# One level of Strassen's scheme for the gate and up products of a streaming encoder layer

## The reference, cut to what matters

```python
h = _rmsnorm(y, norm1_g)
fq, fk, fv, logf, gq, gk, gv, glog, gr = _project(h, w_in, ...)
fox_o = _fox_prompt(...)            # forgetting attention (and _fox_sample)
gla_o, S = _gla_prompt(...)         # gated linear attention
y = y + _merge(fox_o, gla_o, gr, gla_norm_g, w_out)     # silu(gr) gates gla_o
y = y + _swiglu(_rmsnorm(y, norm2_g), w_gate, w_up, w_down)
y = _rmsnorm(y, final_norm_g)

def _swiglu(h, w_gate, w_up, w_down):
    return (jax.nn.silu(h @ w_gate) * (h @ w_up)) @ w_down
```

## Time and profile before

| | us |
|---|---|
| median of 3 runs | 3361.66 (3357.69 to 3363.92) |
| profiled execution | 3358.64 |
| its span (first to last instruction) | 3356.9 |
| busy PE | 3084.2 (92% of the span) |
| busy PE weight loads | 2852.9 (85%) |
| busy DVE | 2053.2 (61%) |
| busy ACT | 1188.7 (35%) |
| busy POOL | 508.0 (15%) |

### The profile page before, as it was taken

How to read it: one execution, slowest core, us unless ns; L and a number is a source line. 1 busy time by engine, 2 the same in 40 slices (tenths; PEclk the granted TensorE clock), 3 DMA queues, 4 the chain that set the end, 5 groups by cost and what they waited for, 6 DMA issues and landing times. The chain is left out here.

```text
span 3356.9 us, 49447 instructions
## 1 busy us (share of the span) xinstructions
PE 3084.2 (92%) x18905; PEld 2852.9 (85%) x18905; DVE 2053.2 (61%) x3540; ACT 1188.7 (35%) x2361; POOL 508.0 (15%) x404
## 2 busy tenths in 40 slices
PE   7999999959999956889978999999998999999996
PEld 5899999947777734677768999999998999999995
DVE  5232212759999833677744666666666666666665
ACT  6353111238888712444432222222224322222223
POOL 0010000000000001321202222222222322222223
PEclk9999999969999977899998999999999999999998
DMA  4235422253242082344435111111133311111112
GB/s 123 73 135 185 148 58 58 51 114 83 63 96 63 1 266 66 111 140 141 144 100 176 51 44 44 50 44 46 48 127 115 107 50 44 44 50 44 44 37 77
DMA packets 280252, 290.37 MB, mean 86 GB/s; under 512 B 32473, under 2 KB 246806, under 8 KB 271040
## 3 DMA queue, kind: packets, MB, share of 16 engines
q1 hardware_dynamic: 277464, 281.12, 28.8%
q10 hardware_dynamic: 1344, 4.36, 0.6%
q0 software_dynamic: 1296, 2.88, 0.3%
HBM read 200.40 MB, written 87.92 MB: 86 GB/s over the span
## 5 line engine op out<-in xcount | busy, mean ns | idle before, releaser
L2376 PE MATMUL ps_ffn<-h,wsp_n 128*128 128x312 f32 (+1 forms) x6336 | 1048.7, 321 | 23.9 <-DMA h<-h2T 23.0
L2376 PEld LDWEIGHTS ps_ffn<-h,wsp_n 128*128 128x128 f32 x6336 | 1011.4, 189 | 27.4 <-issue 23.4
L2302 DVE TENSOR_TENSOR yacc<-ps_ffn,yacc 128x312 f32<-128x312 f32 (+1 forms) x1008 | 489.5, 519 | 386.2 <-PE ps_ffn L2394 386.1
L660 PE MATMUL ps_project<-hT,wsp 128*128 128x416 f32 (+1 forms) x3000 | 602.1, 357 | 0.0
L660 PEld LDWEIGHTS ps_project<-hT,wsp 128*128 128x128 f32 (+1 forms) x3000 | 548.2, 186 | 23.5 <-issue 7.8
L2394 PE MATMUL ps_ffn<-aT,dsp 128*128 128x312 f32 (+1 forms) x3168 | 550.1, 323 | 4.0 <-DVE yacc L2302 3.1
L2394 PEld LDWEIGHTS ps_ffn<-aT,dsp 128*128 128x128 f32 x3168 | 509.5, 189 | 8.0 <-DVE yacc L2302 3.7
L2278 ACT ACTIVATE aT<-a 128x416 fp32r<-128x416 f32 x132 | 65.1, 494 | 821.1 <-DVE a L2353 821.1
L2181 POOL TENSOR_TENSOR wsp_n<-wraw_n,wsp_n 128x1024 fp32r<-128x1024 f32 x88 | 211.8, 2408 | 815.7 <-ACT wsp_n L2222 815.7
L2344 DVE RECIPROCAL silu<-silu 128x416 f32<-128x416 f32 x132 | 304.9, 2310 | 30.1 <-ACT silu L2267 30.0
L1001 ACT ACTIVATE pexp<-ps_fox,ntop 128x512 f32<-128x512 f32 (+2 forms) x320 | 198.6, 621 | 52.9 <-DVE ntop L1044 51.1
(11 more groups left out here) (258 smaller groups left out, 3447.3 us busy)
## 6 DMA issues: line engine op xcount, KB each, us to landing
wraw_n<-in_w_gate_dram SPq DMA_DIRECT2D x44, 512.0 KB, 3.9
wraw_n<-in_w_up_dram SPq DMA_DIRECT2D x44, 512.0 KB, 3.8
draw<-in_w_down_dram SPq DMA_DIRECT2D x44, 512.0 KB, 3.4
h2T<-hT_m SPq DMA_DIRECT2D x16, 1024.0 KB, 5.3
zT<-zs SPq DMA_DIRECT2D x12, 1040.0 KB, 4.1
wraw<-in_w_in_dram SPq DMA_DIRECT2D x24, 512.0 KB, 4.5
h<-h2T SPq DMA_DIRECT2D x8, 1248.0 KB, 12.6
qk_hi<-work SPq DMA_DIRECT2D x8, 1024.0 KB
```

Source lines behind the costliest of these rows:

```text
L660: last = pe.matmul(ps[0:w, p % NB, 0:BLK], wsp[:, b, s, k, 0:w], hT[:, g * TPB:(g + 1) * TPB, v, k, :], start=k == 0 and m == 0, stop=k == ...
L2302: dve.tensor_tensor(y, z, y, ALU.add).then_inc(added, 1)
L2376: last = pe.matmul(ps[:, 2 * q + s, 0:FB[b] * TT], wsp[:, par, s, w, k, :], h2[:, v, k, cols(b)], start=m == 0, stop=m == 3 * KD - 1)
```

## The change

`ffn` is rewritten. The 2080 tokens are taken in four groups of FT = 520 tokens instead of two halves of 1040, and the 22 tiles of D_FF in 11 pairs: 44 pairs of a group and a pair of tiles. For a pair, the gate product is a product of blocks, (2 tiles of 128) x (2 halves of D_MODEL) times (2 halves of D_MODEL) x (2 halves of 260 tokens), and is made by Strassen's scheme in Winograd's form: 7 products of blocks in place of 8. This is an even cell; the up product of the same pair is the odd cell after it (NCELL = 88). Each of the 7 products (P1 to P7, with operands O_B11 ... O_B22) is 4 blocks of 128 rows by 3 passes = 12 matmuls of 260 columns, into one of 6 PSUM banks. The operands are split to high and low parts as before; four of the weight operands are sums of weight blocks, and four of the h operands are sums of h blocks.

The cells' 8 down items (6 matmuls of 260 columns, into 2 PSUM banks) belong to the pair before and stand between the products. At the end of each group (a turn: the last odd cell of groups 0 to 2) the h operands of the next group are made: they exist once, so each is overwritten when the last product that reads it is done. The rows of a finished group are turned, squared, scaled and stored beside the next group's first cells. The weights pass four times, once per group. All is unrolled; `Fori` is gone.

Sigmoid is one ACT instruction in place of Exp, Identity + 1 and DVE's reciprocal, in `ffn` and in `project`'s gate blocks. h2T holds f32 values once, not a high and a low half; `gla_merge` copies h out on ACT (`rows_h`) and has no `low_h`.

The core of the diff, first what other stages lose or get:

```diff
-                    act.activation(silu, ps[:, p % NB, 0:BLK], ACT.Exp, scale=-1.0).then_inc(s_exp, 1)
-                    act.wait_ge(s_exp, m + 1)
-                    act.activation(silu, silu, ACT.Identity, bias=ones[:]).then_inc(s_one, 1)
+                    act.activation(silu, ps[:, p % NB, 0:BLK], ACT.Sigmoid).then_inc(s_sigmoid, 1)
...
-                dve.wait_ge(s_one, m + 1)
-                dve.reciprocal(silu, silu).then_inc(s_inv, 1)
-                dve.wait_ge(s_inv, m + 1)
+                dve.wait_ge(s_sigmoid, m + 1)
...
-            def low_h(c, e):
-                L = width(c)
-                dve.wait_ge(h_high, 2 * c + e + 1)
-                dve.tensor_tensor(hT[:, LO, 4 * e:4 * e + 4, 0:L], ps[:, B_O, :].rearrange("p (k t) -> p k t", k=4)[:, :, 0:L],
-                                  hT[:, HI, 4 * e:4 * e + 4, 0:L].bitcast(F32), ALU.subtract).then_inc(h_low, 1)
```

The new `ffn` on POOL and ACT:

```diff
+            def low_w(c, i):
+                raw = wsum[:, S_OF[i]] if i in S_OF else wraw[:, c % 2, A_OF[i]]
+                pool.wait_ge(w_hi, NPROD * c + i + 1)
+                pool.tensor_tensor(wop[:, i, LO], raw, wop[:, i, HI].bitcast(F32), ALU.subtract).then_inc(w_lo, 1)
...
+            for c in range(NCELL + 1):
...
+                for i in range(NPROD):
+                    if c + 1 < NCELL:
+                        low_w(c + 1, i)
+                    if i == 1 and c:
+                        low_d(c - 1)
+                    if turn and i in (O_B21, O_T3, O_B22):
+                        low_h(q, i)
...
+            def high_w(c, i):
...
+                if c:
+                    act.wait_ge(product, NPROD * (c - 1) + i + 1)
+                act.activation(wop[:, i, HI], raw, ACT.Copy).then_inc(w_hi, 1)
...
+            for c in range(NCELL):
...
+                first_out(c)
+                for i in range(NPROD):
+                    if c + 1 < NCELL:
+                        high_w(c + 1, i)
+                    if turn:
+                        high_h(q, i)
+                    if i == P5 and c:
+                        high_d(c - 1)
+                    if i >= P2:
+                        if s == 0:
+                            gate_sigmoid(u, i - P2)
+                        else:
+                            high_a(u, i - P2)
```

On DVE, the functions and the order of an odd cell:

```diff
+            def sum_w(c, j):
...
+                if c:
+                    dve.wait_ge(w_lo, NPROD * (c - 1) + {0: P5, 1: P6, 2: P7, 3: P3}[j] + 1)
+                if j == 0:
...
+                    dve.tensor_tensor(wsum[:, 0], wraw[:, b, A21], wraw[:, b, A22], ALU.add).then_inc(w_sum, 1)
...
+            def combine(c, what):
...
+                after = {U2: P6, V2: P6, C11: P2, U3: P7, C22: P7, C21: P4, C12: P3}[what]
+                dve.wait_ge(product, NPROD * c + after + 1)
...
+                dve.tensor_tensor(out, product_bank(c, i), partial, ALU.add).then_inc(combined, 1)
...
+            def make_a(u, j):
...
+                dve.tensor_tensor(x, x, sg[:, j], ALU.mult).then_inc(a_made, 1)
...
+            def low_a(u, j):
+                f, t = PLACE[j]
+                dve.wait_ge(a_hi, 4 * u + j + 1)
+                dve.tensor_tensor(aT[:, u % 2, LO, f, t * FH:(t + 1) * FH], cs[:, 1, f, t * FH:(t + 1) * FH],
+                                  aT[:, u % 2, HI, f, t * FH:(t + 1) * FH].bitcast(F32), ALU.subtract).then_inc(a_lo, 1)
...
+                    if turn:
+                        low_h(q, O_B11)
+                        sum_h(q, O_T1)
+                    item(c, 0)
+                    silu(u, J21)
+                    item(c, 1)
+                    if more:
+                        sum_w(c + 1, 0)
+                        sum_w(c + 1, 1)
...
+                    combine(c, U2)
+                    combine(c, V2)
+                    silu(u, J12)
+                    combine(c, C11)
+                    item(c, 2)
+                    item(c, 3)
+                    make_a(u, J11)
+                    combine(c, U3)
+                    combine(c, C22)
+                    make_a(u, J22)
+                    item(c, 4)
+                    low_a(u, J11)
...
+                    item(c, 5)
+                    if more:
+                        sum_w(c + 1, 2)
+                    combine(c, C21)
+                    make_a(u, J21)
+                    low_a(u, J22)
+                    item(c, 6)
+                    if more:
+                        sum_w(c + 1, 3)
+                    combine(c, C12)
+                    make_a(u, J12)
+                    low_a(u, J21)
+                    item(c, 7)
```

`low_a(u, J12)` stands first in the next even cell. `silu` and `gain` are DVE operations on SBUF operands as well. On PE:

```diff
+            def down(n, u, dd, t):
+                h, c = divmod(dd, 4)
+                pe.wait_ge(a_lo, 4 * u + (J12 if t else J21) + 1)
+                pe.wait_ge(d_lo, 2 * u + h + 1)
+                if n >= 2:
+                    pe.wait_ge(item_out, n - 1)
...
+            for c in range(NCELL):
+                cell_product(c, P1)
+                item(c, 0)
+                cell_product(c, P5)
+                item(c, 1)
+                cell_product(c, P6)
+                cell_product(c, P2)
+                item(c, 2)
+                item(c, 3)
+                cell_product(c, P7)
+                item(c, 4)
+                item(c, 5)
+                cell_product(c, P4)
+                item(c, 6)
+                cell_product(c, P3)
+                item(c, 7)
```

More of the change, by code:

```diff
@@ new lines @@
+FT = NTOK // NG4
+FH = FT // 2
+KH = KD // 2
+NPAIR = DFF // (2 * P)
+NPROD = 7
+O_B11, O_T1, O_T2, O_B21, O_T3, O_T4, O_B22 = range(NPROD)
+P1, P5, P6, P2, P7, P4, P3 = range(NPROD)
+A11, A21, A22, A12 = range(4)
+S_OF = {P5: 0, P6: 1, P7: 2, P3: 3}
+A_OF = {P1: A11, P2: A12, P4: A22}
+NBANK = 6
+J11, J22, J21, J12 = range(4)
+PLACE = {J11: (0, 0), J22: (1, 1), J21: (1, 0), J12: (0, 1)}
+NU = NG4 * NPAIR
+NCELL = 2 * NU
+ITEMS = 8
+NROW = FT // TT
+ROW_AFTER = (0, 1, 3, 5, 6)
+LATE = ((0, 1), (2, 3), (4,))
@@ L2158, in last @@
[L2158 to L2168 removed]
+            ws = [d[n][0].rearrange("(k p) f -> p k f", p=P) for n in ("w_gate", "w_up")]
@@ L2170, in _ @@
+            for t in range(NROW):
+                store(NG4 - 1, t)
+            for t in range(NROW):
+                sp.wait_ge(y_stored[t], 16 * (NG4 + (t == NROW - 1)))
         @block.gpsimd
@@ L2284, in _ @@
+            high_d(NCELL - 1)
+            for k, ts in enumerate(LATE):
+                for t in ts:
+                    for half in range(2):
+                        square(NG4 - 1, t, half, late_row(t, half))
+                root(ts, NG4 - 1 + k)
         @block.vector
         def _(dve):
[L2286 to L2302 removed]
@@ new lines, in _ @@
+            low_a(NU - 1, J12)
+            for k in range(ITEMS):
+                add(late_down(0, k), False, k, 0)
+            for k in range(ITEMS):
+                add(late_down(1, k), False, k, 1)
+                if k % 2:
+                    t, half = divmod(k // 2, 2)
+                    row(late_row(t, half), NG4 - 1, t, half)
+            n = NG4 - 1
+            sum_squares(LATE[0], n, 2 * NROW * n + 4)
+            row(late_row(2, 0), n, 2, 0)
+            row(late_row(2, 1), n, 2, 1)
@@ L2413, in step @@
-            def step(u, par, off, gu, down):
-                half = u // NF if isinstance(u, int) and u in (0, NF) else None
-                for slot in range(SLOTS):
-                    if gu:
-                        gate_up(u, par, slot // 2, slot % 2, half)
-                    rows(u, GU, slot)
-                    if down:
-                        downs(u, 1 - par, slot)
-                    rows(u, DN, slot)
-            steps(pe, lambda: None, step, lambda: None)
+            pe.wait_ge(filled, 3)
@@ new lines, in cell_product @@
+            def cell_product(c, i):
+                u, s = divmod(c, 2)
+                q = u // NPAIR
+                pe.wait_ge(w_lo, NPROD * c + i + 1)
+                if c % (2 * NPAIR) == 0:
+                    pe.wait_ge(*h_lows(q, i))
+                if i == P3:
+                    pe.wait_ge(p1_out, c + 1)
+                elif c:
+                    pe.wait_ge(combined, combined_at(c - 1, {P1: V2, P5: U2, P6: C11, P2: C22, P7: C21, P4: C12}[i]))
+                for k in range(KH):
+                    for m, (w, v) in enumerate(PASSES):
+                        last = pe.matmul(product_bank(c, i), wop[:, i, w, k, :], hop[:, i, v, k, :],
+                                         start=k == 0 and m == 0, stop=k == KH - 1 and m == 2)
+                last.then_inc(product, 1)
@@ new lines, in row, with item @@
+            def row(n, t, half, ready):
+                pe.wait_ge(item_out, max(ready, n - 1))
+                for c in range(4):
+                    last = pe.transpose(ps[0:TT, 6 + n % 2, c * P:(c + 1) * P], yacc[:, 4 * half + c, t * TT:(t + 1) * TT], ident[:])
+                last.then_inc(item_done, 1)
+            def item(c, k):
+                if c >= 2:
+                    t, dd = divmod(k, 4)
+                    down(down_item(c, k), c // 2 - 1, 4 * (c % 2) + dd, t)
```

(13 more changed lines are left out.)

773 lines of the change are left out of this document (409 added, 364 removed).

## The result

The changed kernel takes 3377.65 us (median of 6 runs, 3374.66 to 3380.95) against 3361.68 in the same runs: a ratio of 1.0045, with a 95% interval of 1.0035 to 1.0056. It is slower by half a per cent; 3371 had been forecast. The profiled execution took 3378.94 us, its span is 3377.0.

A forecast was written before the change was run, and what follows sets the result against it. PE's matmul issue was taken as the bound: 1408.6 + 90 + 4 + 32.4 − 1580.4 − 31 = −76.4 us, plus 40 x 2.15, gives +9.6 and so 3371 us. Range 3320 to 3391; 8 in 10: 3275 to 3458.

The forecast's parts named there:

- the race: End of odd cell: DVE's low part of a's third quarter against POOL's last low part, within 0.04 us; stall 1.6 or 2.7.
- one matmul of 260 columns: Feed-forward cells: each matmul takes 122.3 ns, so a full cell of 132 takes 16.14 us if PE never waits.
- s: PE's stall per pair before the next even cell's item 0, for DVE's low part of a: 2.15 us, 40 times.
- a turn: At three group changes, stall for h operands, low clock, transposes and gains cost 30 us each, 90 together.
- projection: Gate blocks before the feed-forward part: a chain of 4.8 us becomes 1.3, saving 12 us (0 to −15).
- gla_merge: Two low parts fewer per chunk, 1.1 us each chunk over 16 chunks: −19 us (0 to −22).
- end of gla_merge to first item: Start of feed-forward: first product 4 us later (−5 to +10), then two cells without items at 10.28 us each.
- tail: After the last product: late items, half rows, an addition, gains and a store, 32.4 us against 55.15 (bounds 28 and 40).
- shared way: DVE operations reading two SBUF operands and POOL's operations exclude one another; per pair it is 0.90 to 1.04 full.
- A: Rival, faster: POOL's operations fall into DVE's idle time, no stall per pair, PE stays the bound; 3285 us; chance 0.22.
- B: Rival, slower: each pair stalls 2.7 us and the low clock adds 1.55, 4.25 together; 3455 us; chance 0.20.
- C: Rival: same mechanism, other winner of the race, stall 1.6 us per pair, 3349 us; its side, under 3355, chance 0.18.

The follow-up runs named there:

- the narrow run: Changed kernel with the sums and low parts of h at the three turns made for 8 of 260 tokens: 3337.56 us, ratio 0.9929.
- the experiment with the narrow ones: Kernel before, with gla_merge's low parts of h made for 8 tokens of each chunk from the fourth chunk on: 3353.86 us, ratio 0.9970.
- the version with J21 first: Changed kernel with three DVE steps moved behind the low part of a's third quarter, PE's item 0 asking for two low parts, not three: 3290.77 us, ratio 0.9779.

## Why the prediction came out

The mechanism is the forecast one, in its place: PE waits once per pair, before item 0 of the next even cell, for low J21, because DVE's two-operand operations stand behind POOL's. J21 was foreseen at 19.2 or 20.3 us; it came at 19.40, with low J21 winning the race by 0.03. The terms, by the two profiled executions:

| term | forecast | measured |
|---|---|---|
| one matmul of 260 columns | 122.3 ns | 32.05 us / 264 = 121.4 ns: −10 us in all |
| s | 2.15 | 1.96: −8 over 40 pairs |
| a turn | 30 | 198.04 over five pairs (mean of three turns) − 5 x 32.05 − 4 x 1.96 = 29.95 |
| projection | −12 | 1310.01 − 1323.99 = −14.0 |
| gla_merge | −19 | 417.0 − 429.5 = −12.5 |
| end of gla_merge to first item | 23.05 + 4 + 22 = 49 | 14.97 + 49.05 = 64.0: +15 |
| tail, from the end of the last product | 32.4 | 36.8: +4 |
| slow clock behind ordinary waits, first pair | 0 | +5 |

The deviations add up to some +11 us on 3368.2 (the forecast before the 3.0 for the median); 3378.94 was measured. So the sum is right within 0.3% partly because errors of up to 15 us cancel, and luck has a part in three places.

- The size of s. 2.15 was the middle of two outcomes, 1.6 and 2.7, of which only one could come. Low J21 went first, so the walk's own value was 1.6; J21 then came 0.2 later than walked, and P1 ended 17.48 instead of 17.62 us after the odd cell's start.
- The sign. With s = 1.96 and every other term as forecast, the sum is 3361.7 − 76.4 + 78.4 = 3363.7, which can't be told from no change. That the kernel is slower by 16 us comes from the misses at the start, the tail, gla_merge and the clock, which outweigh those in the matmuls and the projection.
- The turn. Its 30 came out, but not its parts. PE's stretch from the first item of a turn's pair to that of the fifth pair after it:

```profile
2101.34:2299.47 198.13, 173.24 (x1361) 171.05 (x1361) 170.96 (x281) 84.22 (x162) 137.28 (x84) 0.95 0.37 110
```

On the mean of the three turns PE is idle for 24.6 us, 16.8 more than four s, where 15.7 and 6.0 had been forecast for operands and gains; its own work takes 173.4, 13.2 more than five pairs, where 5.2 and 3.1 had been forecast for transposes and the low clock. The stall in front of items 4 and 0 is 13.6 us and belongs to the 17 us of operand work, as the narrow run shows. The gains cost less than their 6.0: of the two later waits, 3.06 and 3.74, which are 2.9 over two s, only the second has a gain in front of it.

The term that was mis-sized most is the start, in two parts that partly cancel. The first product came 14.97 us after gla_merge's last matmul and not 27.05: 12 earlier than forecast and 8 earlier than in the kernel before, where −5 had been the bound. From there to the first item it took 49.05 and not 22: 27 longer. I counted the two cells without items at PE's time alone, 10.28 each. But POOL's list is as long there as in any cell (7 low parts of 1.29 are 9.0 without anything else), with three low parts of h and DVE's sums and low parts of 1040 columns on the same shared way. Of the 27, 9.8 are the wait for low a, 8.1 four waits for h operands (2.20, 2.93, 1.30 and 1.65 us), the first two of them

```profile
1747.15 1.69 PE L2581 MATMUL ps_ffn<-hop,wop 128*128 128x260 f32 x12 [2.20 <-DVE hop L2334]
1751.77 2.64 PE L2581 MATMUL ps_ffn<-hop,wop 128*128 128x260 f32 x12 [2.93 <-DVE hop L2334]
```

and 3.3 two more waits (0.47 and 2.83); the other 5.8 are PE's own 27.8 us, where 22 had been counted at the full clock. The experiment on the start, which takes two cells' reads from POOL, gives 9 of the 27 back; the waits for h operands are 8.9 there, as before.

In gla_merge I counted both low parts of each chunk at full length; the experiment with the narrow ones gives 8.3 in the stage for 13 of 16 chunks, so about 0.65 per chunk and not 1.1. That only one of the two stood in front of PE would explain it; no run moved one alone.

The rivals. A (POOL's operations hidden, s = 0) did not happen in this order of DVE's steps, but its time, 3285, is nearly what the version with J21 first reaches, 3290.8. What I held against it, the shared way being 0.90 to 1.04 full, was no ground: at 32.05 us per pair everything fits, as 240 us of unbroken PE show. The stall needs two things, and each was taken away by itself: POOL's reads, since it goes when POOL writes instead in the same order, and the order, since it goes when the three steps without anything urgent (low J22, the fourth weight sum, make J12) no longer stand in front of low J21. B's stall didn't come, and its price was too high: at s = 3.1 the low clock followed in 16 of 27 cases, 1.0 us per wait on the mean and not 1.55. C had the winner of the race right and missed by 0.36 of s. Of the rule on the shared port, which I cited from the Trainium skill ("SBUF — State Buffer", section "Who interferes with whom"), the trace agrees also for the fourth sum, silu products and making a: 0.69 to 1.49, 0.42 to 0.78 and 0.42 to 0.71 in the rows above, and a sum and the silu products are back at 0.68 and 0.42 where POOL only writes. With the columns/2.4 + 2.5 ns per matmul, which the prediction cited from the Trainium skill ("TensorE: Matmul & The Clock Gate", section "Back-to-back issue gap") and didn't take, the trace doesn't agree: that is 110.8 ns, and measured are 121.4.

## What to carry to other kernels

When work is moved from the engine that bounds to two engines that hold one another up, a table of busy shares isn't enough: walk through the last us before the operand that the bounding engine needs next, with the other engine's operations laid in, and put nothing in front of it that can wait. The order of a few lines was worth 87 us here, more than the 16 us that the change lost. And where a stage has cells with less work for PE, price them by the engine whose list did not get shorter.

## What the hardware showed that I had not expected

Waits of 3.1 us that come every 35 to 38 us were followed by the low clock (0.50, 1.2 GHz) in 16 of 27 cases and not in the others; of 30 waits of 1.93 to 2.06 only two were (after 1929.59 and 3103.84). Before a run I would have taken one length of wait to mean one outcome. And a margin of 0.02 to 0.03 us between two engines held in all 30 pairs: their waits lie within 0.13 us of one another, though the race that decides 1.15 us of them is that close.
